# Turning the softmax weights of a head pair: VectorE's 32x32 block transposes and ScalarE's copies, in place of six turns on TensorE

## What is computed

```python
def block(args):
    q_blk, blk = args
    scores = jnp.einsum('bqhmd,bkhmd->bhmqk', q_blk, k) * scale      # m = 0, 1: two maps per head
    scores = jnp.where(causal, scores, NEG_BIG)
    probs = jax.nn.softmax(scores, axis=-1)
    weights = probs[:, :, 0] - lam * probs[:, :, 1]
    return jnp.einsum('bhqk,bkhe->bqhe', weights.astype(v.dtype), v)
```

## Time and profile before

| | |
|---|---|
| Median of three runs | 961.62 us |
| Profiled execution, its own time | 961.81 us |
| Span from the first to the last instruction of it | 959.8 us |
| Granted TensorE clock, mean | 0.998 |
| PE busy | 942.2 us, 98% |
| DVE busy | 629.6 us, 66% |
| ACT busy | 476.5 us, 50% |
| DMA from memory | 186 GB/s over the span |

### The profile page before, as it was taken

One profiled execution on the slowest core, in us unless ns is written; L12 is line 12 of the kernel. 1 busy time (PEld: TensorE's weight loads), 2 busy tenths in 40 slices (PEclk: granted clock), 3 DMA queues, 4 the chain that ended last, 5 costly groups with the idle time before them and its releaser, 6 DMA issues.

```text
span 959.8 us, 14019 instructions
## 1 busy us (share of the span) xinstructions
PE 942.2 (98%) x5129; PEld 809.8 (84%) x5129; DVE 629.6 (66%) x872; ACT 476.5 (50%) x720; POOL 1.2 (0%) x9
## 2 busy tenths in 40 slices
PE   6999999999999999999999999999999999999996
PEld 5888888888888888888888888888888888888885
DVE  4777656666665666655596447457878878886555
ACT  6866544444434444344465445435465465554441
POOL 0000000000000000000000000000000000000000
PEclk9999999999999999999999999999999999999999
DMA  9666465566666565666566656565655765746562
GB/s 313 218 220 216 143 209 175 175 199 189 203 193 187 188 195 185 207 196 195 183 217 194 192 154 195 159 204 168 197 178 156 221 180 164 206 147 204 191 194 90
DMA packets 149690, 182.30 MB, mean 190 GB/s; under 512 B 8017, under 2 KB 118929, under 8 KB 148881
## 3 DMA queue, kind: packets, MB, share of 16 engines
q1 hardware_dynamic: 148704, 177.25, 59.6%
q10 hardware_dynamic: 944, 4.49, 1.3%
HBM read 176.48 MB, written 2.10 MB: 186 GB/s over the span
## 4 chain that ended last, share of the span: by engine, by line
PE 96%; DVE 1%; ACT 1%; issue 1%; DMA 1%; DVEq 0%; ACTq 0%
PE psum L345 42%; PE psum L346 21%; PE psum L374 9%; PE psum L373 9%; PE psum L372 9%; PE psum L391 1%; PE psum L542 1%; PE psum L416 1%; PE psum L399 1%; DMA cross_gate<-in_mem_norm_dram 1%; PE psum L514 0%; PE psum L408 0%; DVE memT_split L849 0%; PE psum L525 0%; PE psum L524 0%
## 5 line engine op out<-in xcount | busy, mean ns | idle before, releaser
L345 PE MATMUL psum<-hT_split,hi_ring 128*128 128x512 f32 x1600 | 560.0, 396 | 0.0
L821 DVE TENSOR_TENSOR lo_ring<-raw_ring,hi_ring 128x1024 fp32r<-128x1024 f32 x320 | 387.2, 1223 | 251.5 <-ACT hi_ring L591 248.4
L591 ACT ACTIVATE hi_ring<-raw_ring 128x1024 fp32r<-128x1024 f32 x320 | 337.6, 1062 | 401.0 <-PE psum L346 266.2
L346 PE MATMUL psum<-hT_split,lo_ring 128*128 128x256 f32 x1600 | 444.6, 278 | 0.0
L345 PEld LDWEIGHTS psum<-hT_split,hi_ring 128*128 128x128 f32 x1600 | 300.1, 188 | 70.8 <-issue 2.0
L346 PEld LDWEIGHTS psum<-hT_split,lo_ring 128*128 128x128 f32 x1600 | 300.9, 188 | 0.1
L372 PE MATMUL psum<-hi_ring,branchT_split 128*128 128x512 f32 x256 | 99.9, 390 | 0.0
L374 PE MATMUL psum<-hi_ring,branchT_split 128*128 128x512 f32 x256 | 99.6, 389 | 0.0
L373 PE MATMUL psum<-lo_ring,branchT_split 128*128 128x512 f32 x256 | 99.6, 389 | 0.0
L373 PEld LDWEIGHTS psum<-lo_ring,branchT_split 128*128 128x128 f32 x256 | 48.1, 188 | 10.0
L374 PEld LDWEIGHTS psum<-hi_ring,branchT_split 128*128 128x128 f32 x256 | 48.0, 188 | 10.0
(11 more groups left out here) (169 smaller groups left out, 623.7 us busy)
## 6 DMA issues: line engine op xcount, KB each, us to landing
raw_ring<-in_w_in_dram SPq DMA_DIRECT2D x224, 512.0 KB, 4.2
raw_ring<-in_w_out_dram SPq DMA_DIRECT2D x64, 512.0 KB, 4.9
raw_ring<-in_w_kv_mem_dram SPq DMA_DIRECT2D x32, 512.0 KB, 5.5
layer_area<-layer_area SPq DMA_DIRECT2D x48, 64.0 KB, 3.2
stage_area<-in_mem_dram SPq DMA_DIRECT2D x4, 512.0 KB, 7.7
x_residual<-in_x_dram SPq DMA_DIRECT2D x1, 2048.0 KB, 10.7
x_residual<-in_x_dram ACTq DMA_DIRECT2D x1, 2048.0 KB, 8.4
layer_area<-in_post_norm_dram ACTq DMA_DIRECT2D x2, 1024.0 KB, 5.4
```

The source lines that it names most:

```text
L345: mm(o, hi[:, k, P * c:P * (c + 1)], X[:, kt, :], start=kt == 0, stop=False)
L346: last = mm(o[:, SEQ:], lo[:, k, P * c:P * (c + 1)], X[:, kt, 0:SEQ], start=False, stop=kt == KT - 1)
L591: run(whi[:, slot, :], raw[:, slot, :], ACT.Copy).then_inc(hi_ready, 1)
L821: V_.tensor_tensor(wlo[:, slot, :], raw[:, slot, :], whi[:, slot, :].bitcast(f32), SUB)\
```

## The change

PE no longer turns the weights. DVE follows the weights with one instruction that transposes every 32x32 block of the 128 by 2 x 384 weights in place, block by block, into the half of `prob` that held the second map. ACT then copies sixteen pieces, one for each pair of source and target partition group (32 partitions by 2 x 3 x 32 = 192 elements), from there to `probT`. The sixteen copies stand ahead of step 0 of the key group on ACT; `take_values` moves from step 3 to step 2 there. PE's `diff_values` waits for all sixteen.

```diff
+    prob_blocks = prob[:, :, 1, :]
+    QUADRANTS = [(a, b) for a in range(4) for b in range(4)]
@@ tensor
-        def diff_turn(p):
-            pe.wait_ge(w_ready, p + 1)
-            for h in range(2):
-                for b in range(3):
-                    last = nc.tensor.transpose(ps[:, 4 + h, P * b:P * (b + 1)],
-                                               prob[:, h, 0, P * b:P * (b + 1)], ident)
-            last.then_inc(wt_done, 1)
         def diff_values(p):
-            pe.wait_ge(wt_ready, p + 1)
+            pe.wait_ge(wt_ready, p * 16 + 16)
...
             column_group(G + 1, u + B_UNITS, 1 - s, XA,
-                         at={} if first else {2: lambda: diff_turn(p - 1), 3: lambda: diff_values(p - 1)})
+                         at={} if first else {3: lambda: diff_values(p - 1)})
@@ scalar
-        def take_weights(p):
-            act.wait_ge(wt_done, p + 1)
-            run(probT, ps[:, 4:6, 0:3 * P], ACT.Copy).then_inc(wt_ready, 1)
+        def move_weights(p, first, last):
+            act.wait_ge(blocks_turned, p + 1)
+            for a, b in QUADRANTS[first:last]:
+                to = probT.rearrange("p h (k a r) -> p h k a r", k=3, a=4)[32 * b:32 * b + 32, :, :, a, :]
+                block = prob_blocks.rearrange("p h (k b r) -> p h k b r", k=3, b=4)[32 * a:32 * a + 32, :, :, b, :]
+                run(to, block, ACT.Copy).then_inc(wt_ready, 1)
...
             column_group(G + 1, u + B_UNITS, 1 - s,
-                         at={} if first else {2: lambda: take_weights(p - 1), 3: lambda: take_values(p - 1)})
+                         at={} if first else
+                         {0: lambda: move_weights(p - 1, 0, 16), 2: lambda: take_values(p - 1)})
...
         column_group(G_XG1 + 1, U_XG1 + B_UNITS, (G_XG1 + 1) % 2,
-                     at={2: lambda: take_weights(PAIRS - 1), 3: lambda: take_values(PAIRS - 1)})
+                     at={0: lambda: move_weights(PAIRS - 1, 0, 16), 2: lambda: take_values(PAIRS - 1)})
@@ vector, end of softmax_weights
             last.then_inc(w_ready, 1)
+            dve.wait_ge(w_ready, p + 1)
+            V_.transpose(prob_blocks, prob[:, :, 0, :]).then_inc(blocks_turned, 1)
```

More of the change, by code:

```diff
@@ L202, in build @@
     rope_done, s_done, max_ready, exp_done = sem("rope_done"), sem("score_done"), sem("max_ready"), sem("exp_done")
-    w_ready, wt_done, wt_ready = sem("weights_ready"), sem("weights_turned"), sem("weightsT_ready")
+    w_ready, blocks_turned, wt_ready = sem("weights_ready"), sem("weight_blocks_turned"), sem("weightsT_ready")
     pv_done, o_copied, on_ready, n_done, o_taken = sem("pv_done"), sem("o_copied"), sem("o_normed"), sem("o_turned"), sem("o_taken")
@@ L560, in _ @@
         column_group(G_XG1 + 1, U_XG1 + B_UNITS, (G_XG1 + 1) % 2, XA,
-                     at={2: lambda: diff_turn(PAIRS - 1), 3: lambda: diff_values(PAIRS - 1)})
+                     at={3: lambda: diff_values(PAIRS - 1)})
         done0 = PAIRS + 1
```

## The result

The changed kernel takes 983.91 us (median of four, 983.1 to 984.66) against 961.37 (960.96 to 962.53) for the kernel before on the same chip: ratio 1.023, 95% interval 1.0216 to 1.0248. It is 22.5 us slower; 12 were forecast. The profiled execution took 984.03 us, its span is 982.2, its mean granted clock 0.989.

A forecast was written before the change was run, and what follows sets the result against it. PE, 96% of the chain, bounds the kernel; after the change a 39.23 us loop over ACT and DVE exceeds PE's 36.89, putting the last products with the values 11.8 us later: 973.5 us against 961.62, range 963.5 to 982.

The forecast's parts named there:

- The turns leave PE: On PE, six turns of the weights at 0.58 us a pair go away, saving 3.5 us.
- Transposition, 1.1 us with its hops: On DVE after the weights: 0.96 us for the transposition plus an estimated 0.14 for semaphores.
- The copies, p = 0.28: On ACT, sixteen copies start p = 0.28 us apart, 4.5 us for all; each 0.01 of p moves the time 0.8 us.
- The bound from above, 0.40: Upper end for the distance between starts of ACT's copies, 0.40 us; the lower end was 0.16.
- `take_values` at step 2 makes the norm 2.3 us later: DVE's norm starts 5.46 us, not 3.19, after V, where PE starts the products with the values.
- The loop closes at 39.23: Rotary end, mask, weights, transposition, copies, products, rotary end over ACT and DVE: 39.23 us a period against PE's own 36.89.
- The last pair behind tanh: In the last pair ACT's tanh stands ahead of the copies, which start at 866.67, the weights being ready at 862.00.
- PE waits in two places: PE waits 2.3 us a period: before products with values (V) for copies, before scores (S) for the keys' rotary end (R).
- PE waiting at V alone: Sign of being wrong: PE waits only before the products with the values, so the step-2 place of `take_values` costs nothing.
- I add nothing: After the last pair's products with the values start, no further delay is added to the 11.8 us.
- faster, 958: Rival: the ACT and DVE loop isn't the bound, only PE's saving remains, about p = 0.14; 958 us, chance 0.08.
- About even: Rival: the loop is just as long as the saving, p about 0.17; 960 to 963.5 us, chance 0.05.

The follow-up runs named there:

- experiment 9: Changed kernel with one 128x768 copy in place of the sixteen and `take_values` back at step 3: 958.25 us, ratio 0.9965 to the kernel before.
- experiment 4: Changed kernel with each of the sixteen copies within its own partition group, four in a row in the same group: 973.52 us, ratio 1.0129.
- experiment 5: Changed kernel with the copies reordered: target group constant for four copies while the source group changes: 984.7 us, ratio 1.0238.
- experiment 6: Changed kernel with all copies from group g to g + 1, four in a row with the same two groups: 974.69 us, ratio 1.0139.
- experiment 7: Changed kernel with each copy within its own partition group, but another group at every copy: 984.16 us, ratio 1.0241.
- experiment 1: Kernel before with only `take_values` moved to step 2, PE still turning the weights: 968.97 us, ratio 1.0077.
- experiment 2: Changed kernel with `take_values` back at step 3: 977.87 us, ratio 1.0173 to the kernel before.
- experiment 8: Changed kernel with one copy of 128x768 in place of the sixteen: 964.23 us, ratio 1.0029 to the kernel before.
- experiment 10: Changed kernel with GpSimd doing eight of sixteen copies, `take_values` at step 3, the last pair's copies ahead of tanh: 974.19 us, ratio 1.0123.
- experiment 11: Changed kernel with GpSimd doing five copies and ACT eleven, `take_values` at step 3, the last pair's copies ahead of tanh: 961.88 us, ratio 1.0000.

## Why the prediction was wrong, step by step

The mechanism, its two places and the sign were right. Two terms of the sum were not: the distance p of the copies was taken too small, and what follows the last V was taken as nothing. A loop was overlooked as well; it falsified a rival, not the forecast.

- **The turns leave PE, 3.5 us.** Right: 3.3 in experiment 9.
- **Transposition, 1.1 us with its hops.** Right: from the weights' end at 705.74 to the first copy at 706.78 are 1.04, of which 0.06 are hops; the 0.14 put down for them came from no row. The sentence on the Trainium skill's "Vector Engine (DVE) Microarchitecture Reference", section 3.8, holds: 0.98 measured, near its one element per cycle and lane and not near 0.56.
- **The copies, p = 0.28.** This failed. Their price was scaled from rows on 128 partitions whose neighbours all start at the same partition. Those overlap. Copies that change partition group don't, and p is 0.386. Five periods of sixteen copies make 80 x 0.106 = 8.5 us. The first pair, forecast without a wait, waits 1.02. The bound from above, 0.40, held; it was the row nearest in length that misled, since what counted was the change of group from one copy to the next, which no row of before varies. (Copies that overlap are followed after 0.25 us, so for them 0.28 was near.) The Trainium skill's "VectorE: DVE Perf Modes", section on the TRN2 errata, came closer, and I weighed it too low: its 0.35 is near the measured duration of 0.361, still short of the distance. Its section "Two Vector instructions with no wait between them" has VectorE's instructions held back until the earlier ones have finished when an input or the output starts in another group of 32 partitions; experiments 4 to 7 show ACT doing much the same: 0.386 us from start to start, more than the 0.361 of one copy, when either group is another.
- **`take_values` at step 2 makes the norm 2.3 us later.** Right: V + 5.67 against the forecast's V + 5.46, and experiments 1 and 2 price the move at 7.5 and 6.0 us.
- **The loop closes at 39.23.** As a sum it is right: with p as measured it makes 39.23 + 1.70 = 40.93, and 40.81 is the period. The last pair behind tanh: weights ready to copies 872.99 - 868.44 = 4.55, forecast 4.67.
- **"PE waits in two places".** Right, though the profile of the changed kernel hides it, and its sign of being wrong, PE waiting at V alone, nearly seems to be met (14.0 us at V, 2.0 at S). Experiment 7 has copies of the same price and the same time, and there both waits stand open in every period:

```profile
PE psum L516 <- ACT layer_area L766: 14.5, 6, 5.3
PE psum L535 <- DVE layer_area L1096: 5.5, 5, 1.3
```

What differs is the clock. Granted clock by stretch behind the wait of the same pair at V, the changed kernel first (V at 713.07, wait 1.95), then experiment 7 (V at 713.92, wait 1.98):

```profile
715.00:719.00 4.00, 4.00 (x17) 3.42 (x17) 2.77 (x5) 2.56 (x10) 0.00 (x0) 0.67 0.56 168
```

```profile
715.00:719.00 4.00, 4.00 (x26) 3.57 (x25) 2.95 (x3) 3.88 (x12) 0.00 (x0) 1.00 0.42 121
```

In the changed kernel PE works at half its clock for part of this stretch and comes to S that much later, just when the rotary ends: S at 733.41, R at 733.30. In experiment 7 it keeps its clock, comes early, and waits 1.30 us for R (734.00, S at 734.06). Three of the five periods of the changed kernel are of the first kind. So the slow stretch takes the place of the wait at S and costs next to nothing there; the period is 40.8 us in both runs. Why the clock fell in one run and not in the other isn't shown.
- **Behind V: "I add nothing".** This failed: 2.65 us, the clock at half behind the last wait. The prediction named the case ("if it drops behind the last wait, that adds a little") and gave it no price. Behind the last V no wait follows that would take the loss up. The other runs say that it is the clock and not the place of `take_values`. From the last V to the end of the profiled execution are 102.2 us before (961.81 - 859.58), and 102.2 also in experiments 1 and 8 (969.08 - 866.84 and 964.73 - 862.49), which have `take_values` at step 2 and no slow stretch there. In experiments 4 and 7, with about 3.4 us at half behind the last V, they are 103.8 (972.81 - 869.05 and 983.61 - 879.77), and in the changed kernel, with 5.7 us at half, 104.9.
- **Sum.** Of the 10.4 us missed (22.2 against 11.8), 8.5 are copies in five periods, about 1.3 the first pair by the formula, 2.65 the clock, less 2.0 by which the formula overshot: 0.6 in the first pair, 0.5 over four periods, 0.9 in the last. That experiment 4 met 973.5 is in part this luck: its last V is at 869.05, 2.3 before the formula's 871.35, and its tail is 1.5 us longer.
- **The rival "faster, 958", from p = 0.14.** The bound was wrong as put: even with one cheap copy the second loop holds the kernel at 964 (experiment 8). It needs `take_values` at its old place too. "About even", 960 to 963.5, was out of reach for the same reason.

## What to carry to other kernels

Work taken off a saturated engine is worth its time only if every loop that passes through its helpers is shorter than what is left; add up each loop from the profile's rows, those too that go through the busy engine for a part of the way. A step moved forward in a helper's order goes ahead of something: find who waits for that. And before many small instructions take the place of one large, ask not only how long each is but whether the next can overlap it, from rows that alternate the same way. The price of an instruction can also depend on what another engine does beside it, as GpSimd's copies show; a mean over a row of them hides that.

## What the runs showed of the hardware

- ACT's copies of 32x192 float32 within SBUF follow each other by 0.25 us if both partition groups are those of the copy before, by 0.386 if the source or the target group is another (experiments 4 to 7, 4.55 against 6.14 to 6.16 us for sixteen). By the Trainium skill's "ScalarE: Activation LUTs", section "What ACT_TABLE_LOAD costs", an ACTIVATE without pointer operands takes 186 ns and 0.833 per element, and neighbours overlap by about 93: 0.346 and 0.253 here. The trace agrees with both (0.347 median in experiment 4); the overlap is what a change of group takes away.
- DVE's transposition of 32x32 blocks, 128x768 float32, takes 0.98 us.
- GpSimd's copy of 32x192 float32 within SBUF takes 0.34 us, but 1.22 to 1.40 with one of DVE's low halves beside it (an instruction with two inputs in SBUF, 128x1024 float32; experiment 10). So a row of eight takes 6.89 us and a row of five 3.75 (experiment 11), by how many low halves they meet.
- The granted clock was 0.50 for 5.7 us behind a wait of 5.3 us on PE, and 0.67 over four us behind a wait of 1.95; behind a wait of 1.98 in experiment 7 it stayed at 1.00. In experiment 9, without waits, it was 1.00 throughout the pairs. PE's pace halves with it, which costs time only where PE wouldn't have waited anyway.
